# Thirty-two instead of sixteen dense tokens take their down products from gathered rows, in one unbroken run

## What is computed

```python
s = einsum('nhpd,hpkd->nhpk', q, sub_keys)         # 2 x 128 scores a head
s_top, i_top = top_k(s, 16)                        # 16 of each half
best, pos = top_k(cand, 16)                        # 16 of the 256 sums
expert_idx = take_along_axis(cand_idx, pos)        # 128 experts a token
gate = softmax(best)
u = take(expert_down, idx)                         # rows of 1024
a = gelu(einsum('nd,nhkd->nhk', xb, u))
w = gate * a
v = take(expert_up, idx)
y = einsum('nhk,nhkd->nd', w, v)
```

## Time and profile before

| | us |
|---|---|
| median of 3 runs | 1647.79 |
| lowest and highest run | 1645.82, 1649.62 |
| span of the profiled execution | 1645.8 |
| PE busy in it | 1621.5 (99%) |
| DVE busy | 1127.1 (68%) |
| POOL busy | 828.7 (50%) |
| ACT busy | 671.6 (41%) |

### The profile page before, as it was taken

How to read it: one execution, slowest core, us unless ns; L and a number is a source line. 1 busy time by engine, 2 the same in 40 slices (tenths; PEclk the granted TensorE clock), 3 DMA queues, 4 the chain that set the end, 5 groups by cost and what they waited for, 6 DMA issues and landing times.

```text
span 1645.8 us, 26532 instructions
## 1 busy us (share of the span) xinstructions
PE 1621.5 (99%) x9227; PEld 1441.4 (88%) x9227; DVE 1127.1 (68%) x2180; ACT 671.6 (41%) x998; POOL 828.7 (50%) x507
## 2 busy tenths in 40 slices
PE   8999999999999999999999999999999999999998
PEld 6888888788889999999999999998888888888886
DVE  4155441251429999996988888218888888888887
ACT  5342443342434343534444444434333333333333
POOL 4463376413345889996866666766622222222220
PEclk9999999999999999999999999999999999999999
DMA  4222243213435999997999999959999999999992
GB/s 183 98 90 77 79 139 113 92 39 128 154 101 175 332 318 321 300 322 221 343 336 356 357 356 348 324 181 338 397 378 339 346 340 346 342 344 339 351 332 81
DMA packets 152304, 417.97 MB, mean 254 GB/s; under 512 B 15664, under 2 KB 65840, under 8 KB 152112
## 3 DMA queue, kind: packets, MB, share of 16 engines
q1 hardware_dynamic: 89088, 230.33, 40.9%
q0 software_dynamic: 39168, 142.62, 24.5%
q10 hardware_dynamic: 23984, 44.23, 7.0%
HBM read 372.41 MB, written 44.17 MB: 253 GB/s over the span
## 4 chain that ended last, share of the span: by engine, by line
PE 67%; issue 15%; POOL 12%; DMA 3%; DVE 2%; ACT 1%; POOLq 0%; ACTq 0%; DVEq 0%; SPq 0%
PE psum L1464 21%; PE psum L1466 21%; PE psum L1465 21%; POOL w_low L459 9%; PE psum L1759 4%; DMA kept<-down_in 2%; POOL arena L491 2%; DMA hid_dram<-arena 1%; ACT w_high L579 0%; DVE arena L1252 0%; DVE arena L1196 0%; DVE arena L1187 0%; DVE arena L1188 0%; DVE arena L1192 0%; DVE arena L1183 0%
## 5 line engine op out<-in xcount | busy, mean ns | idle before, releaser
L459 POOL TENSOR_TENSOR w_low<-kept,w_high 128x1024 fp32r<-128x1024 f32 x212 | 520.4, 2458 | 370.4 <-ACT w_high L579 369.2
L1464 PE MATMUL psum<-hT_high,w_high 128*128 128x368 f32 (+2 forms) x1408 | 491.5, 349 | 10.1 <-POOL w_low L459 8.2
L1466 PE MATMUL psum<-hT_high,w_low 128*128 128x368 f32 (+2 forms) x1408 | 482.6, 343 | 0.0
L1465 PE MATMUL psum<-hT_low,w_high 128*128 128x368 f32 (+2 forms) x1408 | 482.4, 343 | 0.0
L579 ACT ACTIVATE w_high<-kept 128x1024 fp32r<-128x1024 f32 x212 | 224.1, 1058 | 190.4 <-DMA kept<-down_in 76.8
L1465 PE MATMUL psum<-up_low,wgt_high 128*128 128x512 f32 x768 | 298.8, 389 | 0.0
L1464 PE MATMUL psum<-up_high,wgt_high 128*128 128x512 f32 x768 | 298.8, 389 | 0.0
L1466 PE MATMUL psum<-up_high,wgt_low 128*128 128x512 f32 x768 | 298.8, 389 | 0.0
L1464 PEld LDWEIGHTS psum<-hT_high,w_high 128*128 128x128 f32 x1408 | 264.1, 188 | 29.2 <-POOL w_low L459 13.0
L1466 PEld LDWEIGHTS psum<-hT_high,w_low 128*128 128x128 f32 x1408 | 264.1, 188 | 12.7
L1465 PEld LDWEIGHTS psum<-hT_low,w_high 128*128 128x128 f32 x1408 | 264.4, 188 | 12.3 <-issue 0.5
(11 more groups left out here) (248 smaller groups left out, 1971.1 us busy)
## 6 DMA issues: line engine op xcount, KB each, us to landing
kept<-down_in SPq DMA_DIRECT2D x128, 512.0 KB, 5.9
arena<-up_in SPq DMA_DIRECT2D x128, 512.0 KB, 5.9
kept<-front_w SPq DMA_DIRECT2D x92, 512.0 KB, 3.2
hid_dram<-arena ACTq DMA_DIRECT2D x112, 184.0 KB, 5.7
arena<-hid_dram SPq DMA_DIRECT2D x112, 184.0 KB, 5.1
gate_dram<-arena ACTq DMA_DIRECT2D x40, 512.0 KB, 7.4
under_w<-gate_dram SPq DMA_DIRECT2D x24, 640.0 KB, 8.5
arena<-gate_dram SPq DMA_DIRECT2D x8, 640.0 KB, 8.7
```

The lines of the kernel that those rows point to most:

```text
L459: nc.gpsimd.tensor_tensor(w_low[:, s, :], ring[:, s, :], w_hi[:, s, :].bitcast(F32), ALU.subtract).then_inc(low_ready, 1)
L1464: nc.tensor.matmul(out, lhs[0], rhs[0], start=first, stop=False)
L1465: nc.tensor.matmul(out, lhs[0], rhs[1], start=False, stop=False)
L1466: return nc.tensor.matmul(out, lhs[1], rhs[0], start=False, stop=last)
```

## The change

`EDGE` goes from 16 to 32: 32 tokens are left out of the dense first product, whose width goes to 352. A gather serves 4 experts of each of them, so there are 32 edge gathers and dots, and `ROWS` is 160. In the stream the edge rows stand in one run, 32 to 63 (before, two of every three from 33 to 55), and `EDGE_DONE` is 64 instead of 56. The small moves are 4 instead of 8 in each of the three places, each over 32 partitions. The counts of dots in the choosing (66), in the gate steps (64) and in `DOTS_END` stay.

```diff
-EDGE = 16
+EDGE = 32
 PARTS = P // EDGE
 EDGE_SLOTS = SLOTS // PARTS
 DE = DN - EDGE
 E0, E_BASE = P - EDGE, P - 32
 ROWS = SLOTS + EDGE_SLOTS
-FIRST_EDGE = 33
+FIRST_EDGE = 32
...
     for k in range(ROWS):
-        if edge < EDGE_SLOTS and k >= FIRST_EDGE and k % 3 < 2:
+        if edge < EDGE_SLOTS and k >= FIRST_EDGE:
             stream.append((True, edge))
             edge += 1
...
                     for q in range(PARTS):
-                        if q % 3 == 0:
-                            early_at(EXP_AT[0] + 1 + q // 3)
+                        if q < 3:
+                            early_at(EXP_AT[0] + 1 + q)
                         if q == 0:
                             act.wait_ge(idx_ready, 2)
                         act.dma_start(edge_idx[q * EDGE:(q + 1) * EDGE, :],
...
                 if AHEAD - 6 <= i < AHEAD - 2:
-                    for q in (2 * (i - AHEAD + 6), 2 * (i - AHEAD + 6) + 1):
-                        act.dma_start(edge_back[E0:P, q * EDGE_SLOTS:(q + 1) * EDGE_SLOTS],
-                                      edge_gel[q * EDGE:(q + 1) * EDGE, :]).then_inc(edge_moved, 16)
+                    q = i - AHEAD + 6
+                    act.dma_start(edge_back[E0:P, q * EDGE_SLOTS:(q + 1) * EDGE_SLOTS],
+                                  edge_gel[q * EDGE:(q + 1) * EDGE, :]).then_inc(edge_moved, 16)
```

## The result

The changed kernel takes 1668.22 us (median of 4 runs, 1667.09 to 1669.58) beside 1646.8 for the kernel before (median of 4 runs): a ratio of 1.0132, 95% interval 1.012 to 1.0145. The forecast was 1659.2, the range 1647 to 1672. So the sign and the range held, and the loss is 21.4 us where 11.4 were summed: the time lies near the upper end of the range, where two of the rivals (C at 1668, D at 1667) had been priced as well. Only the trace can tell them apart.

The account below looks back on a forecast made before the run. TensorE, GpSimd and VectorE in turn bound the first 60 blocks, TensorE alone the gate steps. Terms: +5.7 - 7.7 - 3.2 + 13.9 + 2.7 = +11.4 us on the span, forecast 1659.2 us, range 1647 to 1672.

Parts of the forecast that it names:

- C: Last 20 blocks: gathers in the burst land as late as the worst now (8.8), +9.2 on the forecast, 1668; chance 0.12.
- D: Gate steps: held by the DMA engines, they gain nothing, +7.7 on the forecast, 1667; chance 0.12.
- Width: All 128 blocks of the first product: 16 fewer columns save 0.16 us a block, 20.5 us in all as ceiling.
- The gate steps: The 48 gate steps of the first product: whole width gain, 5.45 to 5.29 us a step, -7.7 us.
- E: Matmuls: a floor in the weight load stops the gain, +20 against a forecast with gain, 1670; chance 0.02.
- Choosing: Blocks 0 to 59: added edge dots collide with GpSimd, gate steps begin +5.7 us late; bounds -3 to +15.
- The first term: Choosing: VectorE's chain grows by 16 x 0.86 = 13.8 us; bounds 0 and about 25.
- The second term: Choosing: from the 64th dot, ending near 764, 4.2 us to block 57, then three blocks of 3.84, ending at 779.8.
- Last blocks: Last 20 blocks: -3.2 us by width, but TensorE idles 13.9 us ahead of block 123, behind twelve gathers.
- Clock: After the stall ahead of block 123: the array starts below full speed, +2.7 us; 0 is the other end.
- A: Choosing: edge dots in an unbroken run don't collide, it keeps its 9.6 us; -10.4 in sum, 1637.4; chance 0.10.
- B: Choosing: collisions absorbed, gain limited by GpSimd, -2 in place of +5.7; +3.7 in sum, 1651.5; chance 0.17.

Follow-up runs that it names:

- the second experiment: The changed kernel with 80 instead of 64 rows in the 48 gate steps, 14 left for the last 20 blocks: 1646.16 us, ratio 0.9997.
- the four executions: Profiles of the changed kernel, its two edits of row counts and its filled stall; last turnings at 785.5, 779.6, 784.4 and 778.2 us.
- the run with spread rows: The changed kernel with its last 30 rows two behind each of blocks 108 to 121, one behind 122 and 123: 1657.68 us, ratio 1.0077.
- the run with the filled stall: The changed kernel with 108 added matmuls of 352 columns ahead of block 123, into an unread PSUM bank: 1663.28 us, ratio 1.0111.

## Why the prediction was right, and where it was small

- *Width.* 0.160 us a block, 3.84 and 5.29 us measured. Right. The gate steps gave 8.0 us for 7.7 forecast, and rival D, the DMA engines as the bound there, is out: with 16 more rows, in the second experiment, they carry 388 GB/s in the same time. E is out with the 3.84.
- *Choosing.* The forecast was +5.7 (its own times, 779.8 less 774.35, give 5.5), the profiled execution has +11.2. The mechanism was right: edge dots in collision, VectorE's chain longer, ScalarE's wait for the 64th dot late, block 57 late behind it. The first term is the chain, forecast as 13.8 us: 16 added dots at the mean surplus of the old ones. In this execution 16.7 came, with a mean dot of 2225 ns. But in the four executions with the same program up to this point the means are 2225, 2014, 2119 and 2083 ns and the 64th dot ends 16.7, 10.9, 15.8 and 11.0 us later than before, 13.6 on the mean. So the term was sized well, and the profiled execution is the worst of four draws: how the two engines happen to meet is worth some 7 us at the last turning (778.2 to 785.5). The second term is the way from that dot to the last turning, and it was too small in all four: I counted about 16 us and it took 16.9 to 18.5. It left out 0.55 us of turning between blocks 58 and 59, and in three of the four (18.3 to 18.5) block 57 also began at half the clock (3.4 us of it in the changed kernel, some 1.6 us lost), which I had priced for the last stall alone. And the forecast did not have GpSimd's ring filling up, nor TensorE waiting at the first turning, behind block 39 (2.4 us in two of the four). On the mean of the four the choosing is +7.6.
- *Last blocks.* The stall was forecast as 13.9 us and is 18.05. On the mean of the executions it is the term that missed most, by 4.2 us where the choosing missed by 1.9. Two pieces were small. The burst took 20.6 us from the first gather to the end of the last one (18.8 forecast): with the landings it had, a gather came every 1.7 us. And TensorE had a lead of 1.1 us at block 122 (1092.70 to 1093.79), not 3.6: I took the lead that the kernel before has at its very end, after its rows have run out. With one gather behind every subtraction GpSimd needs 3.55 us of a block of 3.84, so a lead that was lost to one late transfer at block 116 is hardly regained. That was in the rows: 2.41, 0.95 and two short pauses.
- *Clock.* 2.7 forecast from the start of the kernel, 1.96 measured. The clock was at its lower level, 1.2 GHz, when block 123 began after the idle stretch, and at 2.4 GHz again from 1120 us on; with the stretch filled it did not fall. The Trainium skill (TensorE: Matmul & The Clock Gate, Part 1) says that the clock is set by how busy the array has been recently, and the prediction left open whether its price falls due in mid-kernel. It does: this trace agrees.
- *The rivals.* A and B asked whether the choosing would keep or nearly keep its time; both are out with edge dots of 2225 ns, and with a last turning that even in the earliest of the four executions is 3.9 us late. C, late landings, came true in part as the 1.8 us above. Its price was too high: the twelfth gather stands behind two rounds of the ring, so landings of 8.8 instead of 5.5 us add 6.6 and not 9.2. E's figures don't fit each other either: the forecast keeps 11.4 us of width, which gives 1670.6, and not +20. Taken together, +11.2 - 8.0 - 2.9 (width, last 20 blocks) + 18.05 + 1.96 + 0.6 (block 127, which waits for a w_low that is split late) is 20.9 of 21.2 us of span. So the range held with the right mechanism, but part of its width was needed for a scatter that it did not name, that of the choosing.
- The step that was not seen at all is not in the sum but in the design: 30 rows, 26 gathers of them still to issue, are more than GpSimd can place in the last blocks anywhere, while the gate steps had room for them.

## What to carry to other kernels

When a work item is moved from a busy engine to several less busy ones, count each of them per stage and not per kernel: here 16 gathers were free in one stage and cost 22 us in the next. Look at what stands between two instructions of a queue that feeds the critical engine; a rest of a loop ("all that are left") is a burst, and its price is its length less the lead at that point, which must be read at that point. And before adding instructions to an engine that shares memory with another, compare the durations of the same operation with its operand in SBUF and in PSUM: moving one operand was worth as much as the whole change cost.

## What was not expected of the hardware

- The DMA engines carried 388 GB/s, busy all the time (share 1.01), for 253 us with no gate step longer than 5.29 us; 347 GB/s at a share of 0.97 looked like the limit and was not.
- The collision goes both ways, and its price depends on the moment: a dot with both operands in SBUF took from 1.20 to 4.12 us, and each one that was late ended about 1.1 us after a subtraction of GpSimd; gathers that met such dots took 1.76 instead of 0.95 us. Sixteen more dots did not raise the mean clearly: 2014 to 2225 ns in four executions with 32, 2004 and 2073 in two with 16, but 2504 in a third that had its 16 in one run. With the operand in PSUM 32 dots have a mean of 1213 ns and a gather 968.
- A lower clock came not only behind 18 us of idle array but also in the choosing of the changed kernel, behind waits of 2.4 and 2.8 us (a clock of 0.57 from 693 to 697 us and 0.54 from 771.6 to 775.3). It did not come each time. The first matmul of block 57 in the run with spread rows, then in the run with the filled stall:

```profile
765.78 0.63 PE L1464 MATMUL psum<-hT_high,w_high 128*128 128x352 f32 x1 [2.73 <-POOL w_low L459]
...
765.88 0.40 PE L1464 MATMUL psum<-hT_high,w_high 128*128 128x352 f32 x1 [2.73 <-POOL w_low L459]
```

After the same wait of 2.73 us the next matmuls of the first started 0.29 us apart, those of the second 0.16. Why, no run here shows.
